# Two halves of the activations as one 512-column product in the up and gate stages

## The reference, cut to what matters

```
def swiglu(x, w_gate, w_up, w_down):
    return (jax.nn.silu(x @ w_gate) * (x @ w_up)) @ w_down

for l in range(2):
    x = x + 0.5 * swiglu(rmsnorm(x, ffn1_norm[l]), ffn1_w_gate[l], ffn1_w_up[l], ffn1_w_down[l])
    ...
    x = x + 0.5 * swiglu(rmsnorm(x, ffn2_norm[l]), ffn2_w_gate[l], ffn2_w_up[l], ffn2_w_down[l])
```

## Time and profile before

| what | value |
|---|---|
| median of three executions | 2880.54 us (2875.07 to 2881.11) |
| the profiled execution | 2880.22 us |
| its span, first to last instruction | 2878.4 us |
| its mean granted TensorE clock | 0.985 of full speed |
| TensorE matmuls busy | 2786.3 us, 97% |
| GpSimd busy | 1746.0 us, 61% |
| ScalarE busy | 1247.4 us, 43% |
| VectorE busy | 931.4 us, 32% |

### The profile page before, as it was taken

One profiled execution on the slowest core, in us unless ns is written; L12 is line 12 of the kernel. 1 busy time (PEld: TensorE's weight loads), 2 busy tenths in 40 slices (PEclk: granted clock), 3 DMA queues, 4 the chain that ended last, 5 costly groups with the idle time before them and its releaser, 6 DMA issues.

```text
span 2878.4 us, 48414 instructions
## 1 busy us (share of the span) xinstructions
PE 2786.3 (97%) x19981; PEld 2474.1 (86%) x19981; DVE 931.4 (32%) x1833; ACT 1247.4 (43%) x1661; POOL 1746.0 (61%) x1336
## 2 busy tenths in 40 slices
PE   6999999999999999999999999999999999999999
PEld 5766678868888676798999998999999999989999
DVE  3133241341111443434223313354322214354330
ACT  4335442332222345644444444554444434454443
POOL 1402044434454252586986987649897996657896
PEclk8999999999999999999999999999999999999999
DMA  6554433313223245454554557435555557534553
GB/s 207 148 161 144 149 118 88 103 59 103 89 101 103 45 132 162 147 177 134 195 169 148 176 164 207 134 103 175 187 179 166 185 176 179 175 103 150 175 180 126
DMA packets 401892, 418.92 MB, mean 146 GB/s; under 512 B 78890, under 2 KB 371874, under 8 KB 401423
## 3 DMA queue, kind: packets, MB, share of 16 engines
q1 hardware_dynamic: 401712, 416.37, 47.0%
HBM read 415.27 MB, written 3.16 MB: 145 GB/s over the span
## 4 chain that ended last, share of the span: by engine, by line
PE 87%; DVE 4%; ACT 3%; POOL 2%; DMA 2%; issue 1%; SPq 0%; DVEq 0%; POOLq 0%; ACTq 0%
PE ps L906 67%; PE ps L890 17%; POOL ring_r L1778 2%; PE ps L933 2%; DMA ring<-in_w_in 1%; ACT ring_hi L1831 1%; DVE hT_r L3114 0%; DVE stat L2871 0%; SPq L579 0%; ACT arena L2079 0%; DMA ring<-in_w_ada 0%; DVE arena L3324 0%; DVE arena L2885 0%; ACT arena L1891 0%; PE ps L1437 0%
## 5 line engine op out<-in xcount | busy, mean ns | idle before, releaser
L1778 POOL TENSOR_TENSOR ring_r<-ring,ring_hi 128x512 fp32r<-128x512 f32 x1328 | 1743.8, 1349 | 1103.3 <-ACT ring_hi L1831 1069.3
L906 PE MATMUL ps<-hT_r,ring_hi 128*128 128x256 f32 (+1 forms) x6352 | 1164.8, 306 | 27.5 <-DVE hT_r L2619 13.3
L906 PEld LDWEIGHTS ps<-hT_r,ring_hi 128*128 128x128 f32 x6352 | 939.8, 193 | 95.0 <-issue 32.4
L906 PE MATMUL ps<-hT_r,ring_r 128*128 128x256 f32 (+1 forms) x3176 | 707.5, 304 | 0.0
L1831 ACT ACTIVATE ring_hi<-ring 128x2048 fp32r<-128x2048 f32 x312 | 593.6, 1908 | 244.8 <-DMA ring<-in_ffn_w_down 110.8
L906 PE MATMUL ps<-arena_r,ring_hi 128*128 128x256 f32 (+1 forms) x3376 | 561.0, 308 | 7.2 <-DVE arena L3152 3.1
L906 PEld LDWEIGHTS ps<-hT_r,ring_r 128*128 128x128 f32 x3176 | 518.1, 193 | 23.5
L906 PEld LDWEIGHTS ps<-arena_r,ring_hi 128*128 128x128 f32 x3376 | 479.3, 190 | 41.4 <-issue 4.7
L906 PE MATMUL ps<-arena_r,ring_r 128*128 128x256 f32 (+1 forms) x1688 | 314.9, 307 | 0.0
L906 PEld LDWEIGHTS ps<-arena_r,ring_r 128*128 128x128 f32 x1688 | 251.5, 190 | 15.2
L890 PE MATMUL ps<-arena 128*64 128x128 f32 (+9 forms) x1616 | 187.3, 344 | 8.0 <-DVE arena L3296 2.5
(11 more groups left out here) (328 smaller groups left out, 2337.3 us busy)
## 6 DMA issues: line engine op xcount, KB each, us to landing
ring<-in_w_in SPq DMA_DIRECT2D x74, 1024.0 KB
ring<-in_w SPq DMA_DIRECT2D x64, 1024.0 KB
ring<-in_w_ada SPq DMA_DIRECT2D x48, 1024.0 KB
ring<-in_ffn_w_up SPq DMA_DIRECT2D x44, 1024.0 KB
ring<-in_ffn_w_gate SPq DMA_DIRECT2D x44, 1024.0 KB
ring<-in_ffn_w_down SPq DMA_DIRECT2D x44, 1024.0 KB
ring<-in_w_in SPq DMA_DIRECT2D x48, 256.0 KB
ring<-in_w_o SPq DMA_DIRECT2D x8, 1024.0 KB
```

What stands on the lines that cost most here:

```text
L906: last[t] = pe.matmul(o, lhsT, rhs, start=start and j == 0, stop=stop and j == n - 1, skip_group_check=True)
L1778: ins = pool.tensor_tensor(k.ring_lo[s][:, part], k.ring[s][:, part], k.ring_hi[s][:, part], ALU.subtract)
```

## The change

The high and the low activations lie side by side in SBUF. For each weight tile, the two passes that use the high weights (on high and on low activations, 256 columns each) become one matmul of 512 columns, whose result fills a whole PSUM bank: the high half in columns 0 to 255, the low half in columns 256 to 511. The third pass stays 256 columns wide and adds to the first half. ScalarE copies the second half of the bank to SBUF, VectorE adds it to the first half in place, waits for its own sums, and goes on as before. All four feed-forward blocks do this in all 22 up and gate panels; nothing else is changed.

```
+        self.h2_both = hbuf_r[:, 0:2 * KD * SEQ].rearrange("p (x k t) -> p k x t", x=2, k=KD)
...
+A2, A2_HI, SILU2, PLAIN2, LOW2, SQ2, STD2 = 0, 5632, 11264, 12288, 14336, 16400, 18448
...
+            def side_by_side(bs, w, kt):
+                for b, m in zip(bs, range(2)):
+                    mm = pe.matmul(ps[:, b, :].rearrange("p (x t) -> p x t", x=2), w[0][:, kt, m * P:m * P + P], k.h2_both[:, kt],
+                                   start=kt == 0, stop=False, skip_group_check=True)
...
+                return [pe.matmul(ps[:, b, 0:SEQ], w[1][:, kt, m * P:m * P + P], h2[0][:, kt, :], start=False,
+                                  stop=kt == KD - 1, skip_group_check=True) for b, m in zip(bs, range(2))]
...
+            def wide_halves(panels):
+                for _ in range(panels):
+                    w = view(panel(), 0, KD, 256)
+                    bs = [bank() for _ in range(2)]
+                    for kt in range(KD):
+                        mms = side_by_side(bs, w, kt)
+                    for b, mm in zip(bs, mms):
+                        mm.then_inc(k.bank_done[b], 1)
...
             def ffn():
-                normed_panel(h2)
-                wide(1)
+                normed_panel(h2, halves=True)
+                wide_halves(1)
                 with pe.Fori(0, 5) as i, T.loop(i, 5, {"panel": 4, "tiles": 8}):
-                    wide(4)
+                    wide_halves(4)
```

On ScalarE:

```
                 def pair(j, two, first=False):
+                    low = area(LOW2, 2, 4, SEQ)[:, j % 2]
+                    def low_moved(m, b, v):
+                        act.wait_ge(k.bank_done[b], v)
+                        act.activation(low[:, m, :], ps[:, b, SEQ:2 * SEQ], ACT.Copy).then_inc(S["low_moved"], 1)
                     split()
-                    skip(2)
+                    for m in range(2):
+                        low_moved(m, *T.take())
                     if first:
                         deviation()
                     split()
-                    skip(2)
+                    for m in range(2, 4):
+                        low_moved(m, *T.take())
```

On VectorE:

```
+                    for g, (o, tiles) in enumerate(((x, up), (s, [T.take() for _ in range(2)]))):
                         for m, (b, v) in enumerate(tiles):
-                            dve.wait_ge(k.bank_done[b], v)
+                            dve.wait_ge(S["low_moved"], T.next("low_moved"))
+                            ins = dve.tensor_tensor(ps[:, b, 0:SEQ], ps[:, b, 0:SEQ], low[:, 2 * g + m, :], ALU.add)
+                        ins.then_inc(S["tiles_summed"], 1)
+                        dve.wait_ge(S["tiles_summed"], T.next("tiles_summed"))
+                        for m, (b, v) in enumerate(tiles):
                             ins = dve.tensor_tensor(o[:, m, :], ps[:, b, 0:SEQ], rstd2, ALU.mult).then_inc(k.bank_read[b], 1)
```

More of the change, by code:

```diff
@@ L343, in __init__ @@
             "hid_used",
-            "rstd2_ready", "gate1_scaled", "silu_ready", "act2_plain", "act2_rounded", "act2_split", "small_in", "minus_abs_z", "log1p_ready", "decay_ready", "edecay",
+            "rstd2_ready", "gate1_scaled", "low_moved", "tiles_summed", "silu_ready", "act2_plain", "act2_rounded", "act2_split", "small_in", "minus_abs_z", "log1p_ready", "decay_ready", "edecay",
             "cmp_max", "cmp_exp", "cmp_prob", "nsa_max", "nsa_exp", "nsa_prob", "oa_rounded",
@@ L415 @@
 HID, HID_HI, HID_SLOTS = 0, 4 * KD * TOK, 4
-A2, A2_HI, SILU2, PLAIN2, SQ2, STD2 = 0, 5632, 11264, 12288, 16400, 18448
+A2, A2_HI, SILU2, PLAIN2, LOW2, SQ2, STD2 = 0, 5632, 11264, 12288, 14336, 16400, 18448
 (QA, KSLC, KWIN, VSLC, VWIN, GA, KCMP, VCMP, HIDK, ALR, PCT, OA, PROB2, PROBT2, QB, KB, KIN, Z, T1, VB,
@@ L1455, in _, with normed_panel @@
             h2 = k.h2
-            def normed_panel(x):
+            def side_by_side(bs, w, kt):
+                for b, m in zip(bs, range(2)):
+                    mm = pe.matmul(ps[:, b, :].rearrange("p (x t) -> p x t", x=2), w[0][:, kt, m * P:m * P + P], k.h2_both[:, kt],
+                                   start=kt == 0, stop=False, skip_group_check=True)
+                    if fresh[0]:
+                        mm.then_inc(k.panel_begun, 1)
+                        fresh[0] = False
+                return [pe.matmul(ps[:, b, 0:SEQ], w[1][:, kt, m * P:m * P + P], h2[0][:, kt, :], start=False,
[8 more added lines that the diff above has]
+                        mm.then_inc(k.bank_done[b], 1)
+            def normed_panel(x, halves=False):
                 w = view(panel(), 0, KD, 256)
@@ L1463, in normed_panel @@
                     pe.wait_ge(S["h_ready"], T.next("h_ready"))
-                    mms = abreast([ps[:, b, 0:SEQ] for b in bs],
-                                  [tile(w, m, x, ALL)[kt:kt + 1] for m in range(2)], kt == 0, kt == KD - 1)
+                    mms = side_by_side(bs, w, kt) if halves else abreast(
+                        [ps[:, b, 0:SEQ] for b in bs], [tile(w, m, x, ALL)[kt:kt + 1] for m in range(2)], kt == 0, kt == KD - 1)
                     if kt == KD // 2:
@@ L3148, in pair @@
                     x, s = act2[:, two, :], area(SILU2, 2, 2, SEQ)[:, j % 2]
-                    for o, tiles in ((x, up), (s, [T.take() for _ in range(2)])):
+                    low = area(LOW2, 2, 4, SEQ)[:, j % 2]
+                    for g, (o, tiles) in enumerate(((x, up), (s, [T.take() for _ in range(2)]))):
                         for m, (b, v) in enumerate(tiles):
-                            dve.wait_ge(k.bank_done[b], v)
+                            dve.wait_ge(S["low_moved"], T.next("low_moved"))
[3 more added lines that the diff above has]
+                        for m, (b, v) in enumerate(tiles):
                             ins = dve.tensor_tensor(o[:, m, :], ps[:, b, 0:SEQ], rstd2, ALU.mult).then_inc(k.bank_read[b], 1)
@@ L3159, in ffn @@
                 pair(0, slice(0, 2), first=True)
-                with dve.Fori(0, 5) as i, T.loop(i, 5, {"tiles": 8, "silu_ready": 2, "act2_rounded": 2}):
+                with dve.Fori(0, 5) as i, T.loop(i, 5, {"tiles": 8, "silu_ready": 2, "act2_rounded": 2, "low_moved": 8,
+                                                         "tiles_summed": 4}):
                     for j in range(2):
```

## The result

| what | before | after |
|---|---|---|
| median of four executions | 2880.14 us | 2906.58 us (2902.00 to 2908.04) |
| the profiled execution | 2880.22 us | 2902.00 us |
| its span | 2878.4 us | 2900.2 us |

The change is slower: 1.0090 times the time before, 95% interval 1.0078 to 1.0101, some 26 us. The prediction was 2889.7 us with a range up to 2903, so the sign was right and the size was not: it stated 9.5 us.

The account below looks back on a forecast made before the run. TensorE bounds the kernel, GpSimd 10% behind; after the change supply binds. Per block 1.38 us (double pairs) + 1.20 (stage's end) - 0.21 (first gate panel) = 2.37; four blocks add 9.5 to 2880.2: 2889.7 us, range 2871 to 2903.

Parts of the forecast that it names:

- The wide matmul: On TensorE, one 512-column matmul for two of 256 saves 0.0132 us, 0.21 us per panel, which then costs 5.555 us.
- The 1.20 us on the chain: Behind each gate panel, the copies, sums and handoffs start VectorE's old products 1.20 us later.
- The chain as the limit: From gate panel's end through GpSimd to the up panel: 12.43 us against TensorE's 11.11 per pair, so TensorE waits.
- the wait once in two pairs: The supply chain skips a pair, so TensorE waits at every second up panel, some 0.3 to 0.7 us.
- the gate panel's wait behind it: Behind a waited up panel GpSimd needs 5.97 us against TensorE's 5.56, so the gate panel waits near 0.4 us.
- The end of the stage: The first w_down panel's wait for VectorE's last gate products grows from 0.83 to 2.03 us per block, 1.20 more.
- d: Time of VectorE's product of up and gate: forecast 0.89 us, but 1.67 in a block's first two pairs.
- double pair: Two successive pairs of up and gate panels: forecast 23.18 us, 0.12 more than before; five per block.
- rival 2: VectorE's product, issued 0.28 us before GpSimd's boundary, misses it and waits a whole instruction: 2894 to 2902 and over; chance 0.18.
- The locks: VectorE instructions with two SBUF inputs and GpSimd instructions reading SBUF exclude each other, costing GpSimd 0.45 us each time.

Follow-up runs that it names:

- experiment 6: The changed kernel with ScalarE's split of the up panel ahead of Silu and the first w_down step bank by bank: 2860.96 us, 0.9931.
- 11: The kernel before, 256-column products kept, with the split ahead of Silu and the first w_down step bank by bank: 2876.54 us, 0.9990.
- Experiment 5: The changed kernel with the first 128-row step of w_down done bank by bank instead of all eight banks at once: 2901.75 us, 1.0071.
- Experiment 2: The kernel before, 256-column products kept, with the change's copies and sums added (output doubled): 2911.98 us, 1.0108.
- 3: The changed kernel with ScalarE splitting the next but one up panel right after the gate copies, ahead of Silu: 2872.26 us, 0.9970.
- 4: The changed kernel with gate tiles scaled and put through Silu in PSUM, so VectorE's product has one SBUF input: 2874.93 us, 0.9980.
- 12: The changed kernel with the product of up and gate from PSUM and the first w_down step bank by bank: 2864.29 us, 0.9953.
- 9: The changed kernel with the gate tiles' copies and sums over 192 of 256 columns only: 2891.82 us, 1.0050.
- 10: The changed kernel with the gate tiles' copies and sums over 128 of 256 columns only: 2884.72 us, 1.0014.
- experiment 8: The changed kernel with GpSimd's four 512-column instructions per panel cut into eight of 256 columns: 2975.94 us, 1.0331.
- 1: The changed kernel without ScalarE's copies and VectorE's sums, only the 512-column products kept (output incomplete): 2874.18 us, 0.9974.

## Why the prediction was right or wrong

**The wide matmul.** Right: 0.0132 us a merge was forecast. In experiment 6 four matmuls (two wide, two narrow) take 0.697 us, so a merge saves (6 x 0.1201 - 0.697) / 2, about 0.012 us, and a panel takes 5.58 us against 5.555. Five such groups on the chain take 3.48 us:

```profile
2050.05 0.47 PE ps L1461 x2
...
2053.53 0.46 PE ps L1461 x2
```

The Trainium skill (TensorE: Matmul & The Clock Gate, Back-to-back issue gap) states the 2.5 ns for a single, isolated matmul; the prediction set it against a stream, for which that section has other figures. With a saving of 2.5 ns a merge, a panel would have taken 5.73 us, an estimate, and the measurement is against it. Experiments 6 and 11 hold the measured 15.6 us in whole times.

**The 1.20 us on the chain.** Right: from the copies' start (2085.39) to the old products (2086.60) it is 1.21.

**The chain as the limit, the wait once in two pairs, the gate panel's wait behind it.** Right: TensorE waits 1.2 us before an up panel, about 0.2 before the gate panel behind (shown as issue), and then a pair goes without a wait. The end of the panel to TensorE's start took 12.4 us (2085.37 to 2097.79), where the prediction had 11.65.

**The end of the stage.** Right: 2.0 us per block for 0.8, 8.0 - 3.1 = 4.9 us in all, where 4.8 was forecast. Experiment 5 shows that only about half of it can be had back while supply is late.

**The step that failed** is the size of d: "The grant comes 0.08 earlier, so d is 0.69 + 0.20 = 0.89, and two pairs take 23.18". Measured, d is 1.84 and two pairs take 24.23. The working put GpSimd's boundary 0.28 us behind the issue. Counted from GpSimd's start on the waited up panel (2068.41), the issue was forecast at 19.55 and came at 19.65 us; the boundary was forecast at 19.83 and came at 19.64. Two errors of 0.10 and 0.19 us, inside what such a sum over a dozen terms can hold, cost 0.95 us each time. With d = 1.84 the prediction's own sum comes to 24.13 us per double pair and 2905.6 us in all. This is rival 2, which named the place and the 0.28 us but was given 0.18. Its figures, "2894 to 2902 and over", end too low, since 1.67 was taken for the longest that d can be. The double pair is 1.05 us over the forecast. Of this 0.77 stands between the gate panel's end and TensorE's start: 12.42 for 11.65, the 0.95 of d less 0.18 in the chain's other terms. The other 0.28 are in the two panels behind the wait, 6.06 us for 5.97 and 5.75 for 5.56. They are read from the chain, 2097.79 to 2103.85, and from there to 2109.60, where ScalarE's handover begins:

```profile
2103.85 0.72 PE ps L1461 x2
...
2109.62 0.39 ACT arena L2312
```

A double pair 1.17 us longer than before, in place of 0.12, makes the difference. In the second of the four blocks, where the rows so far come from, it was 115.32 us from the first to the last product of up and gate before (2014.94 to 2130.26) and is 120.82 now. The last one before, and the first and the last one now, on VectorE:

```profile
2130.26 1.64 DVE L3154 TENSOR_TENSOR arena<-arena 128x512 f32 x1 [0.70 <-ACT arena L2294]
...
2015.70 1.67 DVE L3189 TENSOR_TENSOR arena<-arena 128x512 f32<-128x512 f32 x1 [0.70 <-ACT arena L2324]
...
2136.52 1.78 DVE L3189 TENSOR_TENSOR arena<-arena 128x512 f32 x1 [0.70 <-ACT arena L2324]
```

That is +5.5 us a block where the prediction had +1.4. With the 1.2 us at the end, four such blocks give 27 us, and the medians differ by 26.4. The profiled executions differ by 21.8. In the change's the first block was milder (118.87 us, first product 0.69), but it had come to that block 5.35 us earlier, in work that the change doesn't touch, and lost 27 us from there on. The first product before, and now:

```profile
1538.10 0.69 DVE L3154 TENSOR_TENSOR arena<-arena 128x512 f32<-128x512 f32 x1 [0.70 <-ACT arena L2294]
...
1532.75 0.69 DVE L3189 TENSOR_TENSOR arena<-arena 128x512 f32<-128x512 f32 x1 [0.70 <-ACT arena L2324]
```

**What shows the cause.** Experiment 2 puts it on the added work, 3 and 6 on its place in ScalarE's order (11 shows that the old kernel gains nothing by that order), 4 and 12 on the product with two SBUF inputs and the Silu ahead of it, which they don't part. That the phase counts, 9 and 10 show; that the product waits longer in the change is read from its trace.

**The locks.** The Trainium skill (SBUF — State Buffer, Who interferes with whom) has the loser of such a meeting wait until the other's instruction is over. The kernel before and the change fit that; experiment 8 (4.01 us beside instructions of 0.70) and three products of experiment 10 don't.

The two traces give more than that. Of their 88 products 78 take the rest of GpSimd's running instruction plus 0.55 us, to within 0.04 us; five meet no GpSimd instruction and take 0.69. The last five are issued 0.04 to 0.06 us before the end of an instruction, within 0.01 us of the start of GpSimd's next, and wait through that next one: 1.84 to 1.85 us. So the longest d beside such instructions could be read off before: 1.30 + 0.55 = 1.85 us, and not 1.67. In experiments 1, 2, 9 and 10 products issued 0.07 to 0.14 us before an end take sometimes 0.69 and sometimes 1.86 to 1.92 us.

## What to carry to other kernels

When a stage's bound is made faster, first read the slack of the chain that feeds it, here 0.3 us, and try to move the feeding instruction ahead of the new work in its engine's order; by that edit alone the same change went from 26 us slower to 9 us faster. Where a chain passes a resource that is granted at another engine's instruction boundaries, a margin of 0.3 us at the end of a sum of a dozen terms isn't a margin: weigh both outcomes, and price the bad one at the other engine's whole instruction. A last result that frees banks for the next stage is on the path even if the stage's middle is covered; taking banks one by one lets the first ones hide it.

## What the runs showed of the hardware that I had not expected

VectorE's instruction with two SBUF inputs can be held up over several back-to-back GpSimd instructions: 4.01 us for 0.69 of work beside ones of 0.70 us, and 2.35 beside ones of 1.25 us (experiments 8 and 10). Otherwise it took the rest of GpSimd's instruction plus 0.55 us. GpSimd's subtraction of 128 x 2048 takes 5.03 us in four instructions and 5.61 us in eight. TensorE was on its way 0.12 us after GpSimd's last instruction here, where the row used for the prediction had 0.23.
